# Where an expert's output rows are added up: results kept in DRAM until the end, or brought to their tokens expert by expert

## The reference, cut to what matters

```python
h = modulate(rmsnorm(x, g_ffn), sh2, sc2)
# each token picks 1 of 4 expert groups, then 2 of the 8 experts in it: 768 (token, expert) pairs
for each of the 32 experts, on the rows of its tokens:
    y = (silu(rows @ w_eg[e]) * (rows @ w_eu[e])) @ w_ed[e]     # 2048 -> 512 -> 2048
moe[token] = sum over its two experts of gate * y[row of the token]
x = x + gate2 * moe
y = rmsnorm(x) * g_final
```

## Time and profile before

| what | value |
| --- | --- |
| median of 3 timed runs | 1829.65 us (1828.02 to 1833.22) |
| profiled execution | span 1835.3 us from its first to its last instruction; a time of its own outside the span is not listed |
| mean granted TensorE clock | 0.976 of full speed |
| TensorE busy, share of the span | 86% |
| VectorE busy | 21% |
| ScalarE busy | 10% |
| GpSimd busy | 9% |
| mean DMA rate | 336 GB/s over the span |

### The profile page before, as it was taken

The page is one execution under the profiler, slowest core; times in us unless marked ns, Lnnn a source line. Parts: engine busy times, 40 slices in busy tenths (PEclk is TensorE's granted clock), DMA queues, the critical chain, the costliest instruction groups (busy, mean ns, idle before and its releaser), DMA issues. The chain is left out here.

```text
span 1835.3 us, 21754 instructions
## 1 busy us (share of the span) xinstructions
PE 1573.0 (86%) x8925; PEld 804.1 (44%) x8925; DVE 391.8 (21%) x879; ACT 191.9 (10%) x518; POOL 165.2 (9%) x358
## 2 busy tenths in 40 slices
PE   5999999999999999978978777777778777778777
PEld 2455454444454444555534343434344434334432
DVE  2012322224242220452111111111111111111115
ACT  3001111111211100110000000000000000000002
POOL 1031000000102020020101101010101010100000
PEclk9999999999999999979989999999999999999998
DMA  9998777656626595379999999999999999999992
GB/s 364 381 308 300 287 275 298 263 221 257 205 69 234 176 229 158 154 270 424 425 427 428 427 427 427 428 428 427 427 426 422 426 426 424 422 426 422 426 389 91
DMA packets 103463, 616.74 MB, mean 336 GB/s; under 512 B 15669, under 2 KB 17829, under 8 KB 67817
## 3 DMA queue, kind: packets, MB, share of 16 engines
q1 hardware_dynamic: 85922, 571.73, 76.7%
q0 software_dynamic: 17488, 44.27, 8.0%
HBM read 602.50 MB, written 34.16 MB: 347 GB/s over the span
## 5 line engine op out<-in xcount | busy, mean ns | idle before, releaser
L1290 PE MATMUL bank<-ring,zbuf 128*64 128x256 f32 x4096 | 474.5, 387 | 154.2 <-DMA ring<-in_w_expert_up 96.3
L1290 PEld LDWEIGHTS bank<-ring,zbuf 128*64 128x64 f32 x4096 | 289.8, 139 | 351.1 <-DMA ring<-in_w_expert_up 120.2
L1313 PE MATMUL bank<-ring,hbuf 128*64 128x512 f32 x1024 | 237.4, 610 | 31.2 <-ACT hbuf L1662 23.0
L853 PE MATMUL bank<-ring,hbuf 128*128 128x512 f32 x384 | 174.2, 599 | 3.0 <-ACT xbuf L1440 2.6
L1313 PEld LDWEIGHTS bank<-ring,hbuf 128*64 128x64 f32 x1024 | 71.2, 140 | 176.3 <-issue 127.7
L849 PE MATMUL bank<-hbuf,ring 128*128 128x384 f32 x384 | 133.8, 495 | 1.2 <-ACT zbuf L1436 0.8
L1153 PE MATMUL bank<-ring,zbuf 128*128 128x512 f32 x288 | 128.7, 602 | 3.1 <-DVE ring L1967 1.9
L853 PEld LDWEIGHTS bank<-ring,hbuf 128*128 128x128 f32 x384 | 70.2, 190 | 83.7 <-issue 82.7
L849 PEld LDWEIGHTS bank<-hbuf,ring 128*128 128x128 f32 x384 | 69.8, 190 | 52.5 <-issue 11.0
L1153 PEld LDWEIGHTS bank<-ring,zbuf 128*128 128x128 f32 x288 | 54.3, 192 | 69.9 <-issue 69.8
L677 POOL CAST cur<-stab 128x1 int32 (+1 forms) x31 | 5.6, 180 | 831.6 <-DVE zbuf L2153 831.6
(11 more groups left out here) (400 smaller groups left out, 1129.6 us busy)
## 6 DMA issues: line engine op xcount, KB each, us to landing
ring<-in_w_expert_up SPq DMA_DIRECT2D x64, 2048.0 KB, 26.9
ring<-in_w_expert_gate SPq DMA_DIRECT2D x64, 2048.0 KB, 26.8
ring<-in_w_expert_down SPq DMA_DIRECT2D x64, 2048.0 KB, 26.1
ring<-in_w_ada SPq DMA_DIRECT2D x96, 1024.0 KB, 7.9
ring<-in_w_in SPq DMA_DIRECT2D x32, 1024.0 KB, 9.0
ring<-in_w_out SPq DMA_DIRECT2D x16, 1024.0 KB, 6.6
y_rows<-modr POOLq DMA_DIRECT2D x1, 6144.0 KB, 22.6
ring<-y_rows SPq DMA_DIRECT2D x3, 2048.0 KB, 22.9
```

The lines of the kernel that those rows point to most:

```text
L853: last = mm(bank[t][:, :], hT[:, k, t * P:(t + 1) * P], w[:, kk_, :], start=(k == 0), stop=(k == KC - 1))
L1290: last = mm(bank[2 + j // 4][64 * q:64 * q + 64, 0:256], xeT[u][:, k % 8, k // 8, :], w[:, kk_, 256 * q:256 * q + 256], start=(k == 0), st ...
L1313: last = mm(bank[5 + n][64 * q:64 * q + 64, :], hidT[u][:, k % 2, k // 2, :], unit(8 + k)[:, 1024 * q + QN * n:1024 * q + QN * n + QN], st ...
```

## The change

The table of results in DRAM goes: no zero fill, no scatter after each expert, no loads back. Instead, `expert_gates` makes `hot` for every expert on VectorE (a copy of one column, L2199 and L2200 again) behind its `y_copy`. During the next expert's `up`, TensorE inserts `combine` after each of the units 0 to 5: two matmuls of `back_to_tokens`, one from the lower and one from the upper partitions, into a pair of PSUM banks (7, 4 and 5, 6 in turn). VectorE's `add_group` multiplies each pair by gate2 and adds it to x: four groups ahead of the gate part of `hidden`, two behind it, all ahead of the multiplication that `hidden` ends with. From the third group on, TensorE waits (`comb_x`) until VectorE has read the banks of the group two before. At the end only the last expert's 12 matmuls and adds are left, in the order 0, 2, 1, 3. The diff, cut to its core:

```diff
             pool.wait_ge(mod_out, 64)
-            link(g.memset(zero, 0.0))
-            g.dma_start(y_dram.rearrange("(p n) (b c) -> p (n b) c", p=P, c=QN),
-                        zero.unsqueeze(1).broadcast_to([P, 8 * NT, QN])).then_inc(y_zero, 16)
...
                     gather(gcur[:, 1 - u, :], 1 - u)
-                    pool.wait_ge(y_v, 2 * i + (u + 1))
-                    pool.wait_ge(y_a, 2 * i + (u + 1))
-                    column(scur[:, u, :], stab, 2 * i + u)
-                    scatter(scur[:, u, :], u)
...
+        LATE_ORDER = (0, 2, 1, 3)
+        GROUP_BANKS = ((7, 4), (5, 6))
...
                     last.then_inc(unit_used, 1)
+                    if between and j < 6:
+                        between(j)
...
+            def back_to_tokens(t, n, b, u=1):
 
                 r = slice(64 * (n // 2), 64 * (n // 2) + 64)
+                return mm(bank[b][:, :], hot[u][r, t * P:t * P + P], ysb[u][r, QN * (n % 2):QN * (n % 2) + QN],
+                          start=True, stop=True)
+
+            def combine(g, u, e):
+
+                if g == 0:
+                    pe.wait_ge(hot_rdy, e + 1)
+                    pe.wait_ge(y_v, e + 1)
+                    pe.wait_ge(y_a, e + 1)
+                if g >= 2:
+                    pe.wait_ge(comb_x, 6 * e + g - 1)
+                for q in range(2):
+                    last = back_to_tokens(g // 2, 2 * q + g % 2, GROUP_BANKS[g % 2][q], u)
+                last.then_inc(comb_ps, 1)
...
+                        up(u, e, e + 1, lambda g: combine(g, 1 - u, 2 * i + (u - 1)))
...
+            pe.wait_ge(last_rdy, 1)
             for t in range(NT):
-                pe.wait_ge(yk_in[t], 16)
-                for n in range(4):
+                for o, n in enumerate(LATE_ORDER):
                     if t == 2:
-                        pe.wait_ge(fin_sum, n + 1)
-                    early_rows(t, n, LATE_BANKS[t][n])
...
+                        pe.wait_ge(fin_sum, o + 1)
+                    back_to_tokens(t, n, LATE_BANKS[t][n]).then_inc(late_ps, 1)
...
+            def expert_gates(u, e):
+
+                link(cp(slot_pair[:, u:u + 1], stab[:, bass.ds(e, 1)]))
+                slot_gates(u)
...
+            def add_group(g, before):
+
+                t, ns = g // 2, (g % 2, 2 + g % 2)
+                dve.wait_ge(comb_ps, before + g + 1)
+                for q, n in enumerate(ns):
+                    last = tt(comb_tmp[2 * (g % 2) + q], bank[GROUP_BANKS[g % 2][q]][:, :], gbc[:, t // 2, QN * n:QN * n + QN], ALU.mult)
+                last.then_inc(comb_x, 1)
+                dve.wait_ge(comb_x, before + g + 1)
+                for q, n in enumerate(ns):
+                    xs = x[:, t, QN * n:QN * n + QN]
+                    tt(xs, xs, comb_tmp[2 * (g % 2) + q], ALU.add)
+
...
+                    if adds:
+                        for n in range(4):
+                            add_group(n, before)
+                    gate_part(u, e)
+                    if adds:
+                        for n in range(4, 6):
+                            add_group(n, before)
                     hidden(u, e)
...
                         rows_copy(1 - u, e + 1)
-                        y_copy(u, e, 16 * i)
...
+                        y_copy(u, e)
...
+                    expert_gates(u, e)
```

More of the change, by code:

```diff
@@ L252, in encoder_step @@
         gate_row = mods_late[:, 768:1536]
-        zero = modr[:, 5, :]
+        hot = [mods_free[:, 2 * TOK + 128:3 * TOK + 128], mods_late[:, 0:TOK]]
         hot2 = kflat
-        yk = [ring[:, 4096 * t:4096 * t + 4096].rearrange("p (k d) -> p k d", k=2) for t in range(NT)]
+        comb_tmp = [hbuf[:, 4096 + QN * n:4608 + QN * n] for n in range(4)]
         sqf = ring[:, 12288:14336]
@@ L465, in _ @@
                         sp.dma_start(unit_pair(j), half_v.rearrange("p e f -> p (e f)")).then_inc(loaded[j], 16)
[L466 to L470, removed]
-            with sp.Else():
[L473 to L478, removed]
+            with sp.Else():
+                sp.nop()
             for t in range(NT):
@@ L1278, in expert_landed, with up @@
                 pe.wait_ge(loaded[j], 16 * loads[j] + 16 + e * 16)
-            def up(u, e, t_need):
+            def up(u, e, t_need, between=None):
                 pe.wait_ge(eT_v, t_need)
@@ L1343, in two_experts @@
                         pe.wait_ge(gates_sb, 1)
-                    up(u, e, e + 1)
+                    if isinstance(i, int) and e == 0:
+                        up(u, e, e + 1)
+                    else:
+                        up(u, e, e + 1, lambda g: combine(g, 1 - u, 2 * i + (u - 1)))
                     if not (isinstance(i, int) and e == NE - 1):
@@ L1363, in _ @@
                                 pe.wait_ge(over_x, 12 * i + 4 * t + n)
-                            back_to_tokens(t, n, 7, True).then_inc(over_ps, 1)
+                            back_to_tokens(t, n, 7).then_inc(over_ps, 1)
                     rows_T(0, e, 16 * 17 + 16 * i)
@@ L1698, in late_squares @@
             def late_squares(t):
-                for n in range(4):
-                    act.wait_ge(fin_sum, 4 * t + n + 1)
-                    act.wait_ge(x1sq, 12 + 4 * t + n)
+                for o, n in enumerate(LATE_ORDER):
+                    act.wait_ge(fin_sum, 4 * t + o + 1)
+                    act.wait_ge(x1sq, 12 + 4 * t + o)
                     af(sqf[:, 0:QN], x[:, t, QN * n:QN * n + QN], ACT.Square, accum_out=x1_parts[:, t, n:n + 1]).then_inc(x1sq, 1)
@@ L2130, in _ @@
             cp(stat[:, 44:45], stat[:, 0:1]).then_inc(tabs, 1)
[L2131 to L2132 removed]
+            ts(stab[:, :], bank[7][:, NE:2 * NE], BIG, None, ALU.add)
             link(stt(rt[:, :, 142:144], rt[:, :, 88:90], float(TOK), rt[:, :, 140:142], ALU.mult, ALU.add))
@@ L2139, in rows_copy, with gate_part @@
                 cp(xeT[u][:, 0:4, :, :].rearrange("p c q s -> p (c q s)"), bank[0][:, :]).then_inc(eT_v, 1)
-            def hidden(u, e):
+            def gate_part(u, e):
                 dve.wait_ge(gu_exp, e + 1)
@@ L2217, in two_experts @@
                     e = 2 * i + u
-                    hidden(u, e)
[L2219 to L2228, removed]
+                    final = isinstance(i, int) and e == NE - 1
+                    adds = not (isinstance(i, int) and e == 0)
+                    before = 6 * (2 * i + (u - 1))
+                    if adds:
[5 more added lines that the diff above has]
+                            add_group(n, before)
+                    hidden(u, e)
+                    if final:
                         last_rows(e)
@@ L2231, in two_experts @@
                         rows_copy(1 - u, e + 1)
-                        y_copy(u, e, 16 * i)
-            peeled(dve, two_experts, NE // 2, link, 6)
+                        y_copy(u, e)
+                    if isinstance(i, int) and e == 0:
+                        dve.wait_ge(iota_rdy, 1)
+                        dve.wait_ge(gates_sb, 1)
+                        dve.wait_ge(gbc_in, 144)
+                    expert_gates(u, e)
+            peeled(dve, two_experts, NE // 2, link, 10)
             dve.wait_ge(ov_rdy, 1)
             n_over = dve.value_load(ov_i[0:1, 0:1], min_val=0, max_val=NOVER)
-            dve.wait_ge(hot_rdy, 1)
+            dve.wait_ge(hot_rdy, NE)
             dve.wait_ge(y_v, NE)
@@ L2275, in add_late @@
             def add_late(t):
-                for n in range(4):
-                    dve.wait_ge(late_ps, 4 * t + n + 1)
+                for o, n in enumerate(LATE_ORDER):
+                    dve.wait_ge(late_ps, 4 * t + o + 1)
                     add_rows(t, n, LATE_BANKS[t][n], fin).then_inc(fin_sum, 1)
-                    if t and n == 0:
+                    if t and o == 0:
                         squares_sum(t - 1)
```

64 lines of the change are left out of this document (18 added, 46 removed).

## The result

The changed kernel takes 1851.7 us (median of 4 runs, 1851.41 to 1853.11) against 1831.43 us before (4 runs, 1828.02 to 1835.99): ratio 1.0106, 95% interval 1.0086 to 1.0126. It is slower by 1.1%; 1849.4 was forecast. The span of the profiled execution is 1850.3 us; 1855 was forecast.

The account below looks back on a forecast made before the run. Bytes bound the loop before, at 30.31 us a round; after, a VectorE and TensorE chain of 31.4 does. 1829.65 + 33.8 (loop) - 14.0 (tail) = 1849.4 us; range 1812 to 1890.

Parts of the forecast that it names:

- What bounds the kernel before: Expert loop before the change: an expert costs what its bytes cost, DMA at 422 to 428 GB/s, 30.31 us a round.
- The term: Scatter removed from the expert loop: its bytes taken as half the software queue's time, 0.53 us an expert.
- the floor of 29.8: Expert loop without the scatter: the shortest round the DMA allows, 29.8 us.
- the chain fits: Rival for the loop: the chain fits and bytes count, rounds of 29.8 to 30.58, 1800 to 1824 us; chance 0.19.
- The chain as the new bound: Loop after: y copy, gates, six groups, `hidden`, `down`, next y copy set the round, taken as 31.4 us.
- The signs that were named: Profile after: DMA about 405 GB/s, weight waits all but gone, TensorE waiting about 1 us for gates, among others.
- Step 4: A group on TensorE: row halves run side by side, a pair is two slots, each group adds 1.26 us.
- The two serial rivals: Pairs on TensorE: instructions queue, round 34.0, 1930 us, chance 0.09; or never side by side, 36.5, 2008 us, 0.04.
- Change of tile shape: TensorE's inserted groups: two changes of shape cost 0.41 us over the slots, per group.
- Both ways equal: Before `down` in a round: VectorE's way takes 24.57 us from J (`down` frees TensorE), TensorE's 24.6; they end together.
- The tail: After the last expert: last multiplication at J (`down` frees TensorE) + 23.9, before 38.03; saves 14 us.
- The span: Profiled execution after: 1855 us, with the 5.65 us that the span before lay over the median taken as unchanged.

Follow-up runs that it names:

- e4: The kernel before without its scatters and the waits for them, results of the first 31 experts left out: 1814.05 us, round 29.65 us.
- e1: The changed kernel with VectorE making an expert's gates' matrix ahead of the y copy, not behind it: 1826.75 us, round 30.61 us.
- e3: The changed kernel without the additions to x of the results of experts 0 to 30: 1843.7 us, round 31.09 us.
- e5: The changed kernel with its six groups in three blocks of two, behind units 0, 2 and 4 of up: 1829.6 us, round 30.60 us.
- e8: The changed kernel with three blocks of two groups, late gates, and no additions to x for experts 0 to 30: 1811.8 us, round 30.04 us.
- e2: The changed kernel with both matmuls of each combine pair from the same row half, not one lower and one upper: 2002.0 us, round 36.20 us.
- e6: The changed kernel with gates' matrix ahead of the y copy and three blocks of two groups: 1802.8 us, ratio 0.9828 to 0.9854 to before.

## Why the prediction was right

- **What bounds the kernel before: right.** Without the scatter the loop followed its bytes (e4). The term was 0.53 and measured 0.66. The forecast that the gain would not be earned after was right too: the round in the middle, 31.37, lies 1.3 above the bytes' 30.05. Wrong was the floor of 29.8. It came from the average of 30.31, which holds the six short rounds at the start; in the middle a round took 30.77 before and 30.07 without the scatter. The forecast of the time was not hurt, since it compared averages with averages; the rival "the chain fits", which counted on rounds down to 29.8, did not allow for that.
- **The chain as the new bound: right.** Its length was taken as 31.4 and measured 31.41. e1, e3, e5 and e8 each took a link out or shortened one, and the round followed: gates 0.80, additions 0.32, changes of shape 1.05. The signs that were named came too: 408 GB/s (405 forecast), no waits for weights, 0.8 us of waiting for the gates (about 1).
- **Step 4, row halves side by side: right** (e2). The two serial rivals fall. By the Trainium skill ("TensorE: Matmul & The Clock Gate", Part 3: Packing small matmuls) matmuls are strict FIFO in start and end. If a matmul's two instructions stand next to each other in the queue, as the prediction takes it, a pair would have taken three slots by that; its 1.13 us, two slots of 0.43 and 0.27, disagree. The order of the four in the queue is not in the profile, so the page is not refuted; that a pair costs two slots is shown.
- **Change of tile shape: right in kind, a little large.** Taken as 0.41 to and fro, measured 0.35 (e3 against e8) and, in single rows, 1.06 + 0.17 - 0.86 = 0.37. It is 2.1 to 2.2 us a round, more than the whole loss. The Trainium skill ("TensorEngine Tiling (Array Packing)", Key Properties) names the drain at a change of mode and the trace agrees, with the 0.35 to 0.37 above; the page gives no price.
- **Both ways equal: right by luck to a tenth.** The sums 24.6 and 24.57 left 0.0; e3 shows VectorE's 0.3 longer, and no row of before could have told such a difference.
- **The tail: right.** 14.0 was taken, 14.8 measured. The 5.6 allowed for a fall of TensorE's clock. The granted clock was 0.67 on average there, but it cost nothing at the start: the first multiplication came at 1820.21 - 1815.08 = 5.13, and the last at 23.2 where 23.9 was forecast.
- **The span: wrong in its offset.** It came 5 us under the forecast, the median 2 over. The forecast had carried the difference between span and median of before (5.65) over as if it belonged to the kernel. In the runs recorded here a span is 1.5 to 1.7 us shorter than the time of the same execution; by that the profiled execution of before took about 1836.9 us (an estimate, 1835.3 + 1.6), 5.5 over the median of the four timed runs, 1831.4. It was one of those that start their experts late (845.79).

The rival "the chain fits" needed a round under 30.58. It describes e6, not this version: two small edits separate them, and either alone ends just above it (30.61 and 30.60).

## What to carry to other kernels

An engine that is a tenth busy can still become the bound, when its new work goes into a loop where another engine waits for its last instruction: sum the chain round the loop, not the busy time. And read a loop's floor from its later rounds: an average over a loop that starts on weights loaded ahead is lower than what its bytes allow (29.65 for 30.05 here). Before placing new work, look where that engine idles in the chain anyway; here three instructions moved ahead of one wait were worth 25 us, and grouping the inserted matmuls, so that the array changes shape 6 times and not 12, about as much again. With both, the version without result rows in DRAM is 1.6% faster than the kernel before (0.9841, interval 0.9828 to 0.9854), where the change as made was 1.1% slower.

## What the runs showed of the hardware that was not expected

- Loads can run at full rate with nobody waiting for them: in e6 the DMA moves 427 GB/s while TensorE waits for no weights. The loop is then faster than its bytes (29.77 for 30.05 us) and uses up what was loaded ahead. The time of a 2 MB load from issue to landing tells it: about 26 us where the bytes bind (before, e4), about 10 where the chain does (after), and growing from 14 to 21 in e6. The rate alone does not tell e6 from e4.
- Two matmuls of 64 rows in different row halves take 1.06 us with their change of shape (start to start), and 1.91 in the same half (e2).
- With the same instructions up to the experts, the first copy of y came between 841.5 and 850.7 us in these executions. The later ones had stretches of a lower granted clock (0.93 to 0.96) with TensorE busy, each worth about 1.6 us. What lowered the clock is open.
